# A residual-and-transpose passage between products, worked in smaller steps, in a two-block transformer on one core

## What is computed

```
# first block
h = rms_norm(x, pre_mix_norm);  proj = h @ w_in            # in1
... differential attention and sparse attention ...
x = x + rms_norm(mix @ w_out, post_mix_norm)               # out1
h = rms_norm(x, pre_ffn_norm)                              # passage n2
u = causal_dwconv(h @ w_up, conv_w, conv_b)                # up1a, up1b
gate, up = jnp.split(u, 2, axis=-1)
y = (gelu(gate) * up) @ w_down                             # down1a, down1b
x = x + rms_norm(y, post_ffn_norm)
# second block
h = rmsnorm(x, mix_pre_gain);   proj = h @ w_in            # passage n3, in2
... sliding-window attention and a gated recurrence ...
x = x + rmsnorm(mixed @ w_out, mix_post_gain)              # out2
h = rmsnorm(x, mlp_pre_gain)                               # passage n4
u = relu(h @ w_up)                                         # up2a, up2b
y = (u * u) @ w_down                                       # down2a, down2b
x = x + rmsnorm(y, mlp_post_gain)
```

## Time and profile before

| | us |
|---|---|
| median of three runs | 2457.21 (2456.75 to 2461.75) |
| the profiled execution | 2461.18 |
| its span | 2459.4 |
| TensorE busy | 2376.5 (97%) |
| VectorE busy | 1461.5 (59%) |
| ScalarE busy | 1148.8 (47%) |
| GpSimd busy | 41.8 (2%) |

### The profile page before, as it was taken

The page is one execution under the profiler, slowest core; times in us unless marked ns, Lnnn a source line. Parts: engine busy times, 40 slices in busy tenths (PEclk is TensorE's granted clock), DMA queues, the critical chain, the costliest instruction groups (busy, mean ns, idle before and its releaser), DMA issues.

```text
span 2459.4 us, 33964 instructions
## 1 busy us (share of the span) xinstructions
PE 2376.5 (97%) x12206; PEld 1991.3 (81%) x12206; DVE 1461.5 (59%) x1849; ACT 1148.8 (47%) x1610; POOL 41.8 (2%) x65
## 2 busy tenths in 40 slices
PE   6999976999999999999999999999999999999997
PEld 5888855888888888888878887778888888888886
DVE  4444366556777545767656677874666544566544
ACT  4444245455555444555445565454544434444442
POOL 1000000000000000000000000000000000000000
PEclk9999888999999999999999999999999999999999
DMA  7666340545655666565647444346566666665652
GB/s 227 193 189 193 104 155 26 171 148 179 187 176 182 200 192 185 176 195 188 205 142 217 135 140 126 95 139 194 157 184 186 191 193 189 188 186 184 210 190 101
DMA packets 311150, 419.19 MB, mean 170 GB/s; under 512 B 15519, under 2 KB 206313, under 8 KB 310293
## 3 DMA queue, kind: packets, MB, share of 16 engines
q1 hardware_dynamic: 308032, 407.09, 54.1%
q0 software_dynamic: 2448, 8.75, 1.1%
q10 hardware_dynamic: 580, 2.20, 0.3%
HBM read 415.86 MB, written 2.12 MB: 170 GB/s over the span
## 4 chain that ended last, share of the span: by engine, by line
PE 86%; issue 7%; DVE 3%; ACT 2%; DMA 1%; POOL 0%; DVEq 0%; SPq 0%; POOLq 0%; ACTq 0%
PE PS L1528 23%; PE PS L1494 12%; PE PS L1492 12%; PE PS L1493 12%; PE PS L1529 11%; PE PS L1724 4%; PE PS L1725 2%; PE PS L1735 1%; PE PS L1737 1%; PE PS L1736 1%; PE PS L1816 1%; DVE x L1080 1%; ACT work L760 1%; PE PS L1802 1%; DMA stage<-in_w_in 1%
## 5 line engine op out<-in xcount | busy, mean ns | idle before, releaser
L1528 PE MATMUL PS<-actT,whi 128*128 128x512 f32 x2432 | 861.4, 398 | 3.2 <-DVE wlo L965 3.2
L936 DVE TENSOR_TENSOR wlo<-stage,whi 128x1024 fp32r<-128x1024 f32 (+1 forms) x367 | 440.1, 1203 | 487.4 <-ACT whi L596 487.4
L1529 PE MATMUL PS<-actT,wlo 128*128 128x256 f32 x2432 | 684.1, 281 | 0.0
L596 ACT ACTIVATE whi<-stage 128x1024 fp32r<-128x1024 f32 (+1 forms) x367 | 381.1, 1042 | 544.5 <-PE PS L1494 519.7
L1528 PEld LDWEIGHTS PS<-actT,whi 128*128 128x128 f32 x2432 | 458.0, 188 | 117.1 <-DVE wlo L965 3.9
L965 DVE TENSOR_TENSOR wlo<-stage,whi 128x1024 fp32r<-128x1024 f32 x298 | 362.8, 1223 | 238.3 <-ACT whi L654 238.1
L654 ACT ACTIVATE whi<-stage 128x1024 fp32r<-128x1024 f32 x298 | 315.9, 1061 | 321.3 <-PE PS L1529 307.6
L1529 PEld LDWEIGHTS PS<-actT,wlo 128*128 128x128 f32 x2432 | 457.3, 188 | 0.1
L1494 PE MATMUL PS<-whi,gT 128*128 128x512 f32 x864 | 340.4, 394 | 0.0
L1493 PE MATMUL PS<-wlo,gT 128*128 128x512 f32 x864 | 338.7, 392 | 0.0
L1492 PE MATMUL PS<-whi,gT 128*128 128x512 f32 x864 | 335.2, 388 | 0.0
(11 more groups left out here) (288 smaller groups left out, 2200.3 us busy)
## 6 DMA issues: line engine op xcount, KB each, us to landing
stage<-in_w_up SPq DMA_DIRECT2D x304, 512.0 KB, 3.8
stage<-in_w_down SPq DMA_DIRECT2D x216, 512.0 KB, 4.5
stage<-in_w_in SPq DMA_DIRECT2D x168, 512.0 KB, 4.5
stage<-in_w_out SPq DMA_DIRECT2D x64, 512.0 KB, 4.6
stage<-in_cmp_k_w SPq DMA_DIRECT2D x8, 512.0 KB, 4.2
stage<-in_cmp_v_w SPq DMA_DIRECT2D x8, 512.0 KB, 5.6
x<-in_x ACTq DMA_DIRECT2D x2, 1024.0 KB, 7.1
grow<-bias_by_distance POOLq DMA_DIRECT2D x2, 1024.0 KB, 7.7
```

Source lines behind the costliest of these rows:

```text
L596: nc.scalar.activation(whi[:, s % SPLITS, 0:wd], stage[:, s % STAGES, 0:wd], ACT.Copy)\
L936: nc.vector.tensor_tensor(wlo[:, s % SPLITS, 0:wd], stage[:, s % STAGES, 0:wd], whi[:, s % SPLITS, 0:wd].bitcast(F32), ALU.subtract).then_ ...
L1528: nc.tensor.matmul(o, whi[:, j % SPLITS, at], actT[:, k, :], start=k == 0, stop=False)
L1529: last = nc.tensor.matmul(o[:, S:2 * S], wlo[:, j % SPLITS, at], actT[:, k, 0:S], start=False, stop=k == KC - 1)
```

## The change

- The residual is added in eight pieces of 512 columns instead of four of 1024. `residual` forms the variance first and multiplies the last 512 columns by the gain while GpSimd works; `residual_pieces(part)` adds two pieces each.
- TensorE transposes in four groups of four chunks, all into banks 4 to 7 (TURN_BANK): groups 0 and 1 before the first tile of the next product, group 2 before its third and group 3 before its fifth tile (`turn_beside`).
- VectorE and ScalarE split chunks 0 to 7 before tile 3 of that product, chunks 8 to 11 behind tile 4 and 12 to 15 behind tile 5; the last two residual pieces stand behind tile 3 on VectorE, the squares of x behind tiles 5, 6 and 7 on ScalarE (`rest_beside`).
- The first block of up1a and up2a, and the first two blocks of in2 together, run in chunk order: two tiles with chunks 0 to 3, two with 4 to 7, and so on. In in2 two feature blocks come first and the key and value block third. Steps that depend on it move: `key_twice` from 12 to 19, `key_turned` from 22 to 24, the transpose of the keys from 19 to 21, the multiply of both first feature blocks with the root row at 14 (`rooted`).
- `idle_matmuls` issues three instead of nine.
- The first tile after in2 that was split in out2 is now split in in2's loop, and splits of mix2's chunks alternate with the last gate steps.
- The result is stored in eight pieces.

```diff
-IN2_BLOCKS = [("tok", C_KA, 256)] + [("feat", C_QA + 256 * i, 256) for i in range(4)]
+IN2_BLOCKS = [("feat", C_QA, 256), ("feat", C_QA + 256, 256), ("tok", C_KA, 256), ("feat", C_QA + 512, 256), ("feat", C_QA + 768, 256)]
...
+IN2_LAST = [6, 7] + [first - 1 for first in IN2_FIRST[3:]] + [87]
...
+TURN_BANK = (4, 5, 6, 7, 4, 5, 6, 7)
...
+    if n < 8:
+        return n % 2, n // 2
...
-        PIECES = [(t, slice(half_ * 1024, (half_ + 1) * 1024)) for half_ in range(2) for t in range(TT)]
+        HALVES = [(t, slice(half_ * 1024, (half_ + 1) * 1024)) for half_ in range(2) for t in range(TT)]
+        PIECES = [(t, slice(part_ * NW, (part_ + 1) * NW)) for part_ in range(4) for t in range(TT)]
+        NP = len(PIECES)
...
-                        src = m[kh * FC * P:(kh + 1) * FC * P, bass.ds(i * step + (c0 + q * other), FW)]
+                        q, kh = (j % 2, j // 2) if by_chunk else (j // (FT // 2), j % (FT // 2))
...
+                first = int(name in ("up1a", "up2a"))
+                if first:
+                    one(0, True)
+                with sp.Fori(first, G[name].blocks) as i:
+                    one(i, False)
...
+            def rest_beside(n, turn):
+
+                def after_tile(j):
+                    if j in (4, 5):
+                        split_turned(turn, range(4 * j - 8, 4 * j - 4), TURN_BANK)
+                    if j >= 5:
+                        squares_of_x(n, ((0,), (1, 2), (3,))[j - 5])
+                return lambda j: after_tile(j + AHEAD)
...
             tok("out1", "squares", then_first="up1a")
-            split_turned("n2")
-            last_up = feat("up1a", True, beside=square_beside(1))
+            split_turned("n2", range(8), TURN_BANK)
+            last_up = feat("up1a", True, beside=rest_beside(1, "n2"))
...
+            split_turned("n3", range(8), TURN_BANK)
+            rest = rest_beside(2, "n3")
...
-                if n < AHEAD + 2 * TT:
-                    squares_of_x(2, (n - AHEAD,))
+                if n < 8:
+                    rest(n - AHEAD)
...
-            split_turned("mix2", range(4, 12), MIX2_BANK)
-            tok("out2", "squares", then_first="up2a", beside=last_chunks)
-            split_turned("n4")
-            last_up = feat("up2a", False, beside=square_beside(3))
+            split_turned("mix2", range(4, 8), MIX2_BANK)
+            gate_sigmoid(1)
+            split_turned("mix2", range(8, 12), MIX2_BANK)
+            tok("out2", "squares", then_first="up2a", beside=last_chunks, skip=AHEAD + 1)
+            split_turned("n4", range(8), TURN_BANK)
+            last_up = feat("up2a", False, beside=rest_beside(3, "n4"))
...
+                    if i is None and b == g.blocks - 1:
+                        return
...
+            def rest_beside(k, turn):
+
+                def after_tile(j):
+                    if j == 3:
+                        residual_pieces(3)
+                    if j in (4, 5):
+                        split_turned(turn, range(4 * j - 8, 4 * j - 4), TURN_BANK)
+                    if j == 7:
+                        root_of_x(k, 0)
+                return lambda j: after_tile(j + AHEAD)
+
+            def first_chunks(turn):
+
+                residual_pieces(0)
+                residual_pieces(1)
+                split_turned(turn, range(4), TURN_BANK)
+                residual_pieces(2)
+                split_turned(turn, range(4, 8), TURN_BANK)
...
+                lastcols = slice(3 * NW, 4 * NW)
+                for t in range(TT):
+                    src = PS[:, 2 + t, 0:NW] if name.startswith("out") else yacc[:, t, lastcols]
+                    last = nc.vector.tensor_tensor(yacc[:, t, lastcols], src, grow[:, lastcols], ALU.mult)
+                if name.startswith("out"):
+                    last.then_inc(ev("acc_free"), 1)
+                    dve.wait_ge(ev("acc_free"), 2 + G[name].acc + 4)
+                else:
+                    me(last)
                 dve.wait_ge(ev("rstd"), n)
...
+            def residual_pieces(part):
+
+                for k in range(TT * part, TT * part + TT):
...
             tok("out1", False, then_first="up1a")
             residual("out1", 3)
+            first_chunks("n2")
             me(nc.vector.memset(pre[:, :, 0:2], 0.0))
-            split_turned("n2")
-            last_up = feat("up1a", True, beside=root_beside(2, 4))
...
-            split_turned("n3")
+            first_chunks("n3")
+            rest = rest_beside(3, "n3")
...
-                if n == 7:
-                    root_of_x(3, 6)
-                if n == 12:
+                if n < 8:
+                    rest(n - AHEAD)
+                if n == 19:
                     key_twice()
-                if n == 22:
...
                     join2(ended)
-            mean_square(0, hstat[:, 0, 8:16], hstat[:, 1, 8:16], P, "o_out", 16)
-            gate_silu(1)
+                    if ended > 1:
+                        rooted(ended)
+                if n == 14:
+                    rooted(0)
+                    rooted(1)
...
-            split_turned("mix2", range(4, 8), MIX2_BANK)
+            split_turned("mix2", range(4, 6), MIX2_BANK)
+            mean_square(0, hstat[:, 0, 8:16], hstat[:, 1, 8:16], P, "o_out", 16)
+            split_turned("mix2", range(6, 8), MIX2_BANK)
+            gate_silu(1)
+            split_turned("mix2", range(8, 12), MIX2_BANK)
             gated(1)
-            split_turned("mix2", range(8, 12), MIX2_BANK)
-            tok("out2", False, then_first="up2a", beside=last_chunks)
...
-            split_turned("n4")
-            last_up = feat("up2a", False, beside=root_beside(5, 11))
+            first_chunks("n4")
+            last_up = feat("up2a", False, beside=rest_beside(5, "n4"))
...
+            for part in range(4):
+                residual_pieces(part)
...
+                    for j in range(FT):
+                        q, kh = (j % 2, j // 2) if first else (j // (FT // 2), j % (FT // 2))
+                        if first:
+                            turn_beside(turned, j)
+                            pe.wait_ge(ev("actlo_" + turned), FC * (kh + 1))
+                        pe.wait_ge(ev("lo_done"), i * FT + (g.first + j + 1 + STAGES))
...
+                if turned is not None:
+                    one(0, 0, True)
+                    one(1, 1)
+                with pe.Fori(int(turned is not None), g.blocks // 2) as r:
...
+            def turn_group(name, grp):
+
+                pe.wait_ge(ev("resid"), NP * RESID[name] + TT * (grp + 1))
+                if grp >= 2:
+                    pe.wait_ge(ev("actlo_" + name), 4 * (grp - 1))
+                for c in range(4 * grp, 4 * grp + 4):
+                    for t in range(TT):
+                        at = (c % 2) * S + t * P
+                        last = nc.tensor.transpose(PS[:, TURN_BANK[c // 2], at:at + P], src_of(name, t, c), ident[:, :])
+                    if c % 2:
+                        last.then_inc(ev("turned_" + name), 1)
+
+            def turn_beside(name, j):
+
+                if j == 0:
+                    turn_group(name, 0)
+                    turn_group(name, 1)
+                if j in (2, 4):
+                    turn_group(name, j // 2 + 1)
...
-                for _ in range(9):
+                for _ in range(3):
...
-            turn("n2", "resid", 0)
             feat("up1a", turned="n2")
...
-            turn("n3", "resid", 4)
...
-                if k == 0:
-                    pe.wait_ge(ev("actlo_n3"), max(4, TC * (j + 1)))
+                if k < 2:
+                    turn_beside("n3", n)
+                    pe.wait_ge(ev("actlo_n3"), FC * (j + 1))
```

## The result

| | before | changed |
|---|---|---|
| median of 4 runs | 2456.98 us | 2477.98 us |
| lowest to highest | 2456.04 to 2461.75 | 2473.51 to 2478.99 |
| profiled execution | 2461.18 | 2478.14 |
| its span, mean granted clock | 2459.4, 0.984 | 2476.4, 0.979 |

The ratio is 1.0081, with a 95% interval from 1.0069 to 1.0093: slower by 21.0 us. The forecast was 2475.0, between 2467 and 2484; the measured median is 3.0 us above it.

What follows compares the result with a forecast made beforehand. TensorE's matmuls were taken as the bound (86% of the chain), with its waits and clock deciding. Terms 2.5 + 8.2 + 5.9 + 2.4 - 0.9 = +18.1 us on the median 2457.21 gave 2475, range 2467 to 2484.

Steps and rivals of the forecast that it cites:

- T earlier: T, the start of the first matmul of the product after a passage, comes 2.8 us earlier.
- The root 21.25 us behind T: GpSimd starts the root of x at T+21.25, before T+14.26 in up1a; there 4.2 us later in time.
- The transfers unchanged: The root's write to DRAM and read back as a row keep their times, 9.47 and 6.56 us in up1a.
- The waits: TensorE waits for weight splits: about 5.5 and up to 3 us in up1a, 8 in in2, 5 in up2a.
- and the clock +1.7: Behind the row waits in in2 and up2a, a lower granted clock costs 1.7 us each.
- First passage, -1.7 for the clock: In up1a the clock loss moves to tile 12, covered by the wait for tile 13's split: -1.7 us.
- Clock at the passages: With three idle matmuls TensorE stands idle 3.0 us and the clock may fall: 0.8 us each, +2.4 for three.
- The end: The last residual starts 0.65 us earlier and the last store is half the size: -0.9 us.
- From in2 to out2, 0: Splits, gate and silu change places, but TensorE's wait there stays: 0 us.
- The rows arrive in time: Rival: root rows cause no waits in the three products, -9 us in all, 2448; chance 0.05.
- Clock: Rival: 1.2 GHz at each passage and for two stretches after each row wait, +26 us, 2483; chance 0.2.
- Chain somewhat shorter: Rival: each root-to-row chain 2 to 4 us quicker, clock held at passages, between +2 and +8 us; chance 0.12.

Runs made afterwards that it cites:

- a_early: Changed kernel with the root of x formed early in all three products (squares ahead of the deferred chunks, variance after tile 5 instead of 7); 2451.47 us.
- b_late: Kernel before with only the variance of x in up1a and up2a moved, after tile 9 instead of tile 7; 2463.5 us.
- a_quiet: a_early with the row's DRAM write and read sent once more behind the residual's root at out1, where no weight loads run; 2451.42 us.
- a_early_idle7: a_early with seven idle matmuls at each passage instead of three; 2450.45 us.
- b_early: Kernel before with the root of x early in up1a and up2a only (variance after tile 5 instead of 7); 2455.81 us.
- a_idle7: Changed kernel with seven idle matmuls at each passage instead of three; 2475.34 us.
- a_row_mm_idle7: Changed kernel with the root row made by diagonal and TensorE instead of through DRAM, and seven idle matmuls; 2446.14 us.
- a_use_later: Changed kernel with VectorE's use of the root row in in2 moved from after tile 14 to after tile 18; 2464.81 us.

## Why the prediction was right, and where it was off

- **T earlier.** Forecast 2.8; measured from the start of the idle matmuls 2.8, 2.1 and 2.5.
- **The root 21.25 us behind T.** Measured 21.6, 21.9 and 21.3. This was the step that decides, and a_early shows it as the cause: with the root at T + 12.0 all three waits are gone.
- **The transfers unchanged.** From the root to VectorE 18.2, 19.4 and 18.3 us, where I had 17.9, 19.5 and 17.3 from before. That was partly luck: that the two transfers vary by 3 us from run to run I had not allowed for; b_late shows what it does (2 to 3 us a product).
- **The waits.** Forecast about 5.5 and up to 3 in up1a, 8 in in2, 5 in up2a; measured 5.8 and 1.3, 7.9, 5.9.
- **By parts.** Passage and first product: forecast 2.5 + 0.8 = 3.3, measured 3.4. in2: 8.2 + 0.8 = 9.0, measured 9.1. up2a with the end: 5.9 + 0.8 - 0.9 = 5.8, measured 7.6. Two terms of up2a were mis-sized. The wait was 5.9 us instead of 5, with the row 18.3 us behind the root and not the 17.3 of before. And the larger one is the clock behind that wait, "and the clock +1.7": it stayed at 1.2 GHz from 1780.5 to 1787.4, and TensorE worked in that from 1781.2 on, 6.2 us, which costs 3.1. In in2 it was low as long, from 1326.6 to 1333.4, but TensorE still waited until 1330.4, so 1.5 us was lost there, about what I had. The sum was 18.1 us, the parts show 20.1, the medians 21.0.
- **First passage, -1.7 for the clock.** Right that the low clock moves under the wait for tile 13: after 5.84 us TensorE ran tile 12 at 0.50, and then waited only 1.30.
- **Clock at the passages.** Forecast 2.4 for three; four more idle matmuls gave back 2.6 by the medians. The parts show 5.7, of which 3.1 are quicker transfers, and with the early root 1.0 by the medians and 2.9 by the parts. So the size is right within what can be told.
- **The end.** From the start of TensorE's last matmul to the end of the span 13.83 us before, 13.05 after: -0.8 of the -0.9.
- **From in2 to out2, 0.** TensorE's wait there was 3.5 us and is 3.5.

The rivals: "The rows arrive in time" needed a chain of 12.3 us from GpSimd's start to VectorE's release; almost without a load beside it, the chain takes 14.1 by the same count (517.61 to 531.7 in a_quiet). What that rival said of the rest was about right: its -9, with the clock kept at the passages, is -7.5 by the medians and -9.6 by the parts in a_early_idle7, where no wait for a weight split is left in the three products. "Clock" came true in part: the clock fell at each passage and behind the waits it was low for two of my stretches, but only in up2a did most of that fall on work. "Chain somewhat shorter" didn't happen in this run, but did in b_late.

## What to carry to other kernels

When work is deferred into the first block of a product, ask what else on its engines hangs on that block: here four chunks on ScalarE put off a square, a root and a row that was already the last to arrive in up1a, and the gain of 2.8 us at the start became a loss of 21. A wait in the stream of an engine that feeds another should stand where the data are used or later, not where the code reads best: four splits moved ahead of it took 7 us off in2. A row made from columns of 128 values came sooner by a diagonal and TensorE (4.9 us) than through DRAM (18); in the time this was worth as much as an early root, and no more could be shown.

## What the runs showed of the chip that I had not expected

- With a DMA share of 0.01 and less from 520 to 528 us, GpSimd's write of two columns of 512 bytes took 8.1 us with its issue, though the share was 0.00 in its last 4 us. The read back to 128 partitions took 5.0, the last 1.5 of them beside loads. Their length isn't mostly contention.
- How long TensorE must stand idle for the clock to fall was not sharp. An idle time of 2.42 us at in2's passage kept 1.00 in the kernel before and in b_late, and lost it in b_early; one of 1.8 us there kept it in a_idle7 and lost it in a_row_mm_idle7 (0.85 and 0.72 from 1270 to 1278); 2.8 us lost it at two passages of the changed kernel and 4.2 at the third; 3.0 us in up2a of b_late, at a split, kept it.
- Behind waits of 5.8 to 7.9 us the clock was at 1.2 GHz for 6.8 us, behind 2.8 for 3.4, though TensorE was busy all the time from 1784 on in up2a, where it was still low until 1787.4 (0.58 from 1784 to 1788). The length of the wait doesn't settle it: the wait of 3.5 us in out2 was followed by 3.4 us at 1.2 GHz in the kernel before and in the changed one, and by 6.8 in a_early, a_quiet and a_use_later.
- The same program up to the first passage took from 513.9 to 521.7 us in the profiled runs.
